# Sparse-expert ranking with four score chunks and four row dots per head, selectors made on VectorE alone, three score chunks per 32 tokens of one-hots

## The reference

```python
def peer(h, w_query, sub_keys, expert_u, expert_v):          # 8 heads, 128 keys, top 16
    qry = (h @ w_query).reshape(B, S, PEER_HEADS, 2, PEER_HALF)
    sc = jnp.einsum('bshpd,hpnd->bshpn', qry, sub_keys)
    top_s, top_i = lax.top_k(sc, K)
    cand = top_s[..., 0, :, None] + top_s[..., 1, None, :]
    best, flat = lax.top_k(cand.reshape(B, S, PEER_HEADS, K * K), K)
    ...
    experts = i1 * 128 + i2                                   # of 16384, 128 per token
    g = softmax(best)
    ...
        act = gelu(einsum('td,tkd->tk', xt, expert_u[et])) * gt
        return einsum('tk,tkd->td', act, expert_v[et])
```

## Time and profile before

| what | us |
|---|---|
| median of 3 runs (1989.82 to 1993.12) | 1991.67 |
| the profiled execution's own time | 1990.13 |
| its span in the profile | 1988.5 |
| TensorE busy (matmuls) | 1825.9, 92% of the span |
| VectorE busy | 1345.9, 68% |
| ScalarE busy | 697.0 |
| GpSimd busy | 649.0 |

### The profile page before, as it was taken

One profiled execution on the slowest core, in us unless ns is written; L12 is line 12 of the kernel. 1 busy time (PEld: TensorE's weight loads), 2 busy tenths in 40 slices (PEclk: granted clock), 3 DMA queues, 4 the chain that ended last, 5 costly groups with the idle time before them and its releaser, 6 DMA issues.

```text
span 1988.5 us, 24521 instructions
## 1 busy us (share of the span) xinstructions
PE 1825.9 (92%) x8747; PEld 1510.3 (76%) x8747; DVE 1345.9 (68%) x2464; ACT 697.0 (35%) x1072; POOL 649.0 (33%) x418
## 2 busy tenths in 40 slices
PE   5899999989979999778888699999999999999996
PEld 4555555558758999777777599999999999877774
DVE  5423233244446999679999487777767888777776
ACT  2241514252334444333333233333333333333333
POOL 0000000000004665676666354444434444322320
PEclk7989888889989999899999899999999999999998
DMA  7413030202313332347888898888878888899992
GB/s 317 169 45 146 21 127 21 84 21 96 111 49 125 124 123 88 117 161 200 218 222 226 243 406 314 309 301 308 310 274 320 318 307 300 312 326 332 325 326 101
DMA packets 217066, 409.64 MB, mean 206 GB/s; under 512 B 111792, under 2 KB 143536, under 8 KB 213040
## 3 DMA queue, kind: packets, MB, share of 16 engines
q1 hardware_dynamic: 170928, 254.56, 37.6%
q0 software_dynamic: 37440, 142.62, 20.9%
q10 hardware_dynamic: 8640, 11.80, 1.6%
HBM read 369.87 MB, written 39.06 MB: 206 GB/s over the span
## 4 chain that ended last, share of the span: by engine, by line
PE 65%; DVE 18%; DMA 6%; issue 4%; ACT 4%; POOL 2%; SPq 1%; DVEq 0%; ACTq 0%; POOLq 0%
PE bank L781 22%; PE bank L725 17%; PE bank L687 6%; DMA u_raw<-euT 4%; PE bank L580 4%; PE bank L621 3%; DVE hot_j L1354 3%; PE bank L615 2%; DVE hot_i L1354 2%; PE bank L584 1%; DVE rows L1335 1%; ACT v_split L1052 1%; PE bank L609 1%; DVE u_split L1330 1%; PE bank L634 1%
## 5 line engine op out<-in xcount | busy, mean ns | idle before, releaser
L725 PE MATMUL bank<-h_split,u_split 128*128 128x384 f32 x3072 | 566.2, 341 | 26.2 <-DVE u_split L1330 15.1
L725 PEld LDWEIGHTS bank<-h_split,u_split 128*128 128x128 f32 x3072 | 545.2, 191 | 33.5 <-DVE u_split L1330 15.4
L781 PE MATMUL bank<-v_split,a_split 128*128 128x512 f32 x2304 | 544.8, 392 | 4.9 <-DVE a_split L1383 3.6
L781 PEld LDWEIGHTS bank<-v_split,a_split 128*128 128x128 f32 x2304 | 427.7, 188 | 104.6 <-issue 18.4
L496 POOL DMA_INDIRECT rows<-ev,idx x128 | 173.7, 1357 | 311.6 <-DVE row_sum L1346 265.5
L496 POOL DMA_INDIRECT rows<-eu,idx x128 | 177.0, 1383 | 232.4 <-DVE dots L1335 212.6
L1052 ACT ACTIVATE v_split<-v_raw 128x1024 fp32r<-128x1024 f32 x128 | 135.8, 1061 | 211.7 <-PE bank L781 208.5
L949 ACT ACTIVATE gelus<-bank 128x384 f32<-128x384 f32 x128 | 62.9, 491 | 388.6 <-PE bank L725 388.5
L1366 DVE TENSOR_TENSOR v_split<-v_raw,v_split 128x1024 fp32r<-128x1024 f32 x128 | 156.6, 1224 | 22.2 <-ACT v_split L1052 22.0
L1335 DVE CUSTOM_DVE_ANT_0 rows<-rows,h_rows 128x1024 f32<-128x1024 f32 x128 | 165.9, 1332 | 0.9 <-DMA rows<-eu,idx 0.8
L1346 DVE SCALAR_TENSOR_TENSOR row_sum<-rows,agate,row_sum 128x1024 f32<-128x1024 f32 x127 | 162.7, 1281 | 5.3 <-DVE row_sum L1346 0.5
(11 more groups left out here) (208 smaller groups left out, 2119.1 us busy)
## 6 DMA issues: line engine op xcount, KB each, us to landing
u_raw<-euT SPq DMA_DIRECT2D x128, 512.0 KB
v_raw<-ev SPq DMA_DIRECT2D x128, 512.0 KB
arena<-w_ada SPq DMA_DIRECT2D x12, 2048.0 KB, 8.0
gates_scratch<-stage SPq DMA_DIRECT2D x12, 2048.0 KB, 17.9
gates<-gates_scratch SPq DMA_DIRECT2D x128, 192.0 KB
arena<-w_units SPq DMA_DIRECT2D x24, 512.0 KB, 3.5
gelu_scratch<-gelus ACTq DMA_DIRECT2D x60, 192.0 KB, 2.0
gelus<-gelu_scratch SPq DMA_DIRECT2D x60, 192.0 KB
```

What stands on the lines that cost most here:

```text
L725: last = pe.matmul(ps[6 + b][:, 0:TD], us[:, b, wp, k * P:(k + 1) * P], hs[:, xp, k, 0:TD], start=(k == 0 and q == 0), stop=(k == DC - 1 a ...
L781: last = pe.matmul(ps[2 * t + f][:], ar[:, b, ap, t * P:(t + 1) * P], vs[:, b, vp, f * 512:(f + 1) * 512], start=(first and q == 0), stop= ...
```

## The change

- Ranking: four score chunks per head instead of three, then four instead of eight (EARLY = 36). The turns go with chunks 0 to 4 rather than heads 0 to 4. The row index is computed head by head (`row_index`), and 28 row dots come early: four ahead of each rank from head 2 on, four after rank 7; their gathers stand on GpSimd at the end of each head from 1 on. VectorE's loop over heads is written out.
- One-hots: GpSimd's multiplication goes. VectorE makes `ohj` by one `tensor_scalar` per token (compare with the index, multiply by the gate, both one scalar per partition), `ohi` as before. Three score chunks, with 3, 3 and 2 groups of four tokens behind them, share 32 tokens: 36 chunks in place of 24. A dot comes in every third. VectorE works five groups ahead. TensorE's loop is written out.
- 76 chunks are stashed instead of 60, so 52 instead of 68 iterations have a new score chunk. 48 dots lie before the values instead of 32, the other 80 in 28 iterations; rows of `expert_v` are added from iteration 29, 64 of them by iteration 52.

```diff
-EARLY = 32
-GSTEPS = TD // 16
-STASHED = EARLY + GSTEPS + 4
+PER_HEAD = 4
+EARLY = PER_HEAD * HEADS + 4
+GROUPS = TD // 4
+BESIDE = 3 * GROUPS // 8
+STASHED = EARLY + BESIDE + 4
-DOTS_G = 32
-DOTS_BY = 38
-ACC_FROM = 39
-ACC_F = 76
+DOTS_HEAD = 4
+DOTS_RANK = DOTS_HEAD * (HEADS - 1)
+DOTS_G = DOTS_RANK + GROUPS // 8 + 8
+DOTS_BY = 28
+ACC_FROM = 29
+ACC_F = 64
+def groups_after(c):
+    k = c - EARLY
+    first = 8 * (k // 3) + 3 * (k % 3)
+    return range(first, first + (3, 3, 2)[k % 3])
...
 @block.sync
+            for n in range(GROUPS // 16):
+                for k in range(6):
+                    u_load(EARLY + RING + 6 * n + k)
+                for b in range(4):
+                    sp.wait_ge(staged[b], 4 * (n + 1) + FREE)
...
 @block.gpsimd
+                if g < P and g % TOPK == 0:
+                    pool.wait_ge(idx_ready, g // TOPK + 1)
...
+                u_low(PER_HEAD * n + 2)
+                u_low(PER_HEAD * n + 3)
                 if n:
                     index_picks(n - 1)
                 if n + 2 < HEADS:
                     query_low(n + 2)
+                u_low(PER_HEAD * n + 4)
+                u_low(PER_HEAD * n + 5)
+                if n:
+                    for k in range(DOTS_HEAD):
+                        gather(DOTS_HEAD * (n - 1) + k)
...
-            for s in range(GSTEPS):
-                for b in range(4):
-                    t0 = 16 * s + 4 * b
-                    pool.wait_ge(hot_eq[b], 2 * s + 2)
-                    nc.gpsimd.tensor_tensor(ohj[:, b, :, :], ohj[:, b, :, :], slotsT[:, 2, t0:t0 + 4].unsqueeze(2).to_broadcast([P, 4, P]),
-                                            ALU.mult).then_inc(hot_ready[b], 1)
-                gather(NG + s)
 @block.tensor
+            for c in range(EARLY, EARLY + BESIDE):
+                scores(c, c % 2)
+                for g in groups_after(c):
+                    b = g % 4
+                    pe.wait_ge(hot_ready[b], g // 4 + 1)
+                    pe.wait_ge(staged[b], g // 4 + FREE)
+                    for q in range(4):
+                        last = pe.matmul(ps[2 + b][:, q * P:(q + 1) * P], ohj[:, b, q, :], ohi[:, b, q, :], start=True, stop=True)
+                    last.then_inc(hot_done[b], 1)
 @block.scalar
+            for c in range(EARLY, EARLY + BESIDE):
+                gelu(c)
+                u_high(c + 2)
+                gelu_stash(c)
+                for g in groups_after(c):
...
 @block.vector
             def rank(i, finish_before=False):
+                if i >= 2:
+                    for k in range(DOTS_HEAD):
+                        dot(DOTS_HEAD * (i - 2) + k)
...
                 if finish_before:
                     finish(i - 1)
+                    row_index(i - 1)
...
+            for i in range(HEADS):
+                rank(i, finish_before=i > 0)
+            for k in range(DOTS_HEAD * (HEADS - 2), DOTS_RANK):
+                dot(k)
             finish(HEADS - 1)
...
+            def hot(g):
+                b = g % 4
+                if g >= 4:
+                    ve.wait_ge(hot_done[b], g // 4)
+                nv.tensor_tensor(ohi[:, b, :, :], cst[:, K_IOTA:K_IOTA + P].unsqueeze(1).to_broadcast([P, 4, P]),
+                                 slotsT[:, 0, 4 * g:4 * g + 4].unsqueeze(2).to_broadcast([P, 4, P]), ALU.is_equal)
+                for q in range(4):
+                    t = 4 * g + q
+                    ins = nv.tensor_scalar(ohj[:, b, q, :], cst[:, K_IOTA:K_IOTA + P], slotsT[:, 1, t:t + 1], slotsT[:, 2, t:t + 1],
+                                           ALU.is_equal, ALU.mult)
+                ins.then_inc(hot_ready[b], 1)
+            for g in range(5):
+                hot(g)
+            ve.wait_ge(u_split, EARLY + 2)
+            for c in range(EARLY, EARLY + BESIDE):
+                u_low(c + 2)
+                if (c - EARLY) % 3 == 2:
+                    dot(DOTS_RANK + (c - EARLY) // 3)
+                for g in groups_after(c):
+                    if g + 5 < GROUPS:
+                        hot(g + 5)
```

More of the change, by code:

```diff
@@ L403, in _ @@
             for n in range(HEADS):
-                u_load(3 * n + 4)
+                u_load(PER_HEAD * n + RING)
                 if n + 2 < HEADS:
@@ L742, in _ @@
                     key_scores(n)
-                scores(3 * n, 3 * n % 2)
-                if n:
-                    key_scores(n)
-                if n < TT:
-                    turn(n, x, n)
-                elif n == TT:
-                    turn(n, h, TT - 1)
-                scores(3 * n + 1, (3 * n + 1) % 2)
-                scores(3 * n + 2, 3 * n % 2)
-            for c in range(3 * HEADS, EARLY):
+                for k in range(PER_HEAD):
+                    c = PER_HEAD * n + k
+                    scores(c, c % 2)
+                    if n and k == 0:
+                        key_scores(n)
+                    if c < TT:
+                        turn(c, x, c)
+                    elif c == TT:
+                        turn(c, h, TT - 1)
+            for c in range(PER_HEAD * HEADS, EARLY):
                 scores(c, c % 2)
@@ L760, in _ @@
                 last.then_inc(slotsT_done, 1)
-            with pe.Fori(0, GSTEPS // 2) as r:
-                for e in range(2):
-                    scores(r * 2 + (EARLY + e), e)
-                    for b in range(4):
-                        pe.wait_ge(hot_ready[b], r * 2 + (e + 1))
-                        pe.wait_ge(staged[b], r * 2 + e + FREE)
-                        for q in range(4):
-                            last = pe.matmul(ps[2 + b][:, q * P:(q + 1) * P], ohj[:, b, q, :], ohi[:, b, q, :], start=True, stop=True)
-                        last.then_inc(hot_done[b], 1)
-            for c in range(EARLY + GSTEPS, STASHED + 1):
+            for c in range(EARLY, EARLY + BESIDE):
+                scores(c, c % 2)
+                for g in groups_after(c):
[5 more added lines that the diff above has]
+                    last.then_inc(hot_done[b], 1)
+            for c in range(EARLY + BESIDE, STASHED + 1):
                 scores(c, c % 2)
@@ L1238, in _, with dot @@
                 nv.tensor_tensor(hs[:, 1, k, :], h[:, k, :], hs[:, 0, k, :].bitcast(F32), ALU.subtract).then_inc(h_split, 1)
+            def dot(k):
+                ve.wait_ge(rows_in[k % NG], 16 * (k // NG + 1))
+                nv.tensor_tensor_reduce(rows[k % NG], rows[k % NG], hT, 1.0, 0.0, ALU.mult, ALU.add, dots[:, k:k + 1]).then_inc(rows_used, 1)
             def finish(i):
@@ L1309, in rank @@
                                      ALU.is_equal).then_inc(picks, 1)
[L1311 to L1315 removed]
+            for i in range(HEADS):
+                rank(i, finish_before=i > 0)
+            for k in range(DOTS_HEAD * (HEADS - 2), DOTS_RANK):
+                dot(k)
             finish(HEADS - 1)
[L1320 removed]
             ve.wait_ge(slots_ready, HEADS)
             nv.tensor_copy(gate3[:], slots[:, 2, TT - 1, :])
[L1323 removed]
+            row_index(HEADS - 1)
             ve.wait_ge(slotsT_ready, 3)
[L1325 removed]
             def u_low(c):
@@ L1330, in u_low @@
                 nv.tensor_tensor(us[:, c % 2, 1, :], ut[:, c % RING, :], us[:, c % 2, 0, :].bitcast(F32), ALU.subtract).then_inc(u_split, 1)
-            def dot(k):
-                ve.wait_ge(rows_in[k % NG], 16 * (k // NG + 1))
-                nv.tensor_tensor_reduce(rows[k % NG], rows[k % NG], hT, 1.0, 0.0, ALU.mult, ALU.add, dots[:, k:k + 1]).then_inc(rows_used, 1)
             def add_row(k):
```

117 lines of the change are left out of this document (40 added, 77 removed).

## The result

| | us |
|---|---|
| before, median of 9 runs | 1991.94 |
| after, median of 9 runs (1995.36 to 2002.02) | 1999.14 |
| ratio after to before, 95% interval | 1.0034 (1.0023 to 1.0045) |
| the profiled execution of after, and its span | 1996.83, 1995.1 |

The account below looks back on a forecast made before the run. TensorE, busy 92%, was taken as the bound, losing 76 us in one-hots paced by VectorE. Stretch ending at 1123.6 with 66.9 us more done than at 1110.6: 53.9 ahead, less 2.9, 51.0; forecast 1941, range 1930 to 1968.

Parts of the forecast that it names:

- Step 1: One-hots: selectors on VectorE alone at 0.26 us each, unit 17.8 us, so TensorE at 19.5 sets the pace.
- Rival A: One-hots: VectorE sets the pace, selectors 0.32 to 0.35 us or held by gathers; 1950 to 1972, chance 0.14.
- Step 2: One-hots: 36 chunks, 235.1 us of work, plus 21 us of TensorE stops behind stage writes; stretch 258.1 us.
- the 2 us for the start: One-hots: 2 us added at their start because u_low(36) stands behind the last index_picks on GpSimd.
- Step 3: Ranking: four chunks per head, VectorE's period 30.5 us (29.4 to 32), slots turned at 865.5, a gain of 1.1.
- four dots at 1.14: Ranking: four early dots per head at 1.14 us each, part of VectorE's 30.5 us period.
- Steps 4 and 5: Values: dots moved forward cost 0 (up to 19 us), at 330 GB/s; sixteen more stashed chunks cost 2.9 us.
- Rival C: Stretch after 1155: DMA limits it, adding 19 us for 1960; chance 0.08.
- Step 6: Tail from 1111 to 1155 stays, with SP's last two writes again ahead of a load.
- D: Ranking: contended dots and gather waits make the period 39.7 us, not 30.5; slower, 2000; chance 0.06.
- E: Loss only moves from one-hots to the ranking's end, VectorE's period near 38, time within 4 us; chance 0.04.
- rival B: One-hots: the stall on the stage writes vanishes, with fewer gathers per round; 1920 to 1930, chance 0.06.

Follow-up runs that it names:

- e5: e3 with one more u_load issued ahead of each pair of stage writes, in the three-chunk order; 1939.47 us, ratio 0.9728.
- e8: Kernel before with selectors on VectorE alone and one u_load moved ahead of each pair of stage writes; 1944.68 us, ratio 0.9763.
- e2: After, with each rank's four dots moved from ahead of it to behind its candidate sums, the last four left in place; 1961.89 us, ratio 0.9861.
- e3: e2 with the last four ranking dots done among the one-hots; 1962.87 us, ratio 0.9851.
- e11: After without early dots in the ranking; 1957.88 us, ratio 0.9829.
- e1: After, with its 28 early dots replaced by a sum over the same row, one SBUF operand instead of two; 1944.04 us, ratio 0.9763.
- e6: e5 without early dots in the ranking; 1930.24 us, ratio 0.9685.

## Why the prediction was wrong, point by point

- **Step 1 (selectors), right.** The 384 `tensor_scalar` take 340 ns in the middle, and four of them in a row 1.11 us, so they start 0.26 us apart, the value that the prediction took. TensorE waits for `hot_j` 2.3 us in all. GpSimd's gathers didn't hold them. Rival A is out.
- **Step 2 (three chunks, and the wait behind the stage writes), right in sum and in mechanism, off in its parts.** The stretch lasted from 922.75 to 1180.37, 257.6 us against 258.1 forecast. In each round there is one ScalarE wait for `u_raw` (7.50 us; 8 to 10 forecast) and a TensorE stop (1.98 and 0.77; 4.2 forecast), and pairs of writes come 42.9 us apart ((1181.37 - 966.68)/5; 43 forecast). e5 and e8 show the cause. By start times a round loses 3.5 us (42.9, less six chunks at 4.25 and 16 groups at 0.87), 17.5 in all and not 21, and the 2 us for the start don't show. What makes up for it was in no term: chunks take 4.25 us from start to start (937.52 - 933.27) rather than 4.18, and after 23 us of idling TensorE starts the stretch at half its clock (0.50 granted from 922 to 925, 0.70 from there to 931), so that its first chunk takes 6.10. That the sum came within 0.5 us is luck in part. Rows of after, of the selectors' line first, then from the timeline:

```profile
L1361 DVE TENSOR_SCALAR hot_j<-cst,slots_turned x384: 329/340/435, 926.9 to 1176.3; 128x128 f32<-128x128 f32 x192
...
991.80 1.06 ACT L944 ACTIVATE u_split<-u_raw 128x1024 fp32r<-128x1024 f32 x1 [7.50 <-DMA u_raw<-euT]
...
993.49 1.13 PE L773 MATMUL bank<-hot_i,hot_j 128*128 128x128 f32 x8 [1.98 <-ACT stage L1040]
1001.34 1.16 PE L773 MATMUL bank<-hot_i,hot_j 128*128 128x128 f32 x8 [0.77 <-DVE hot_j L1361]
1180.37 3.89 PE L729 MATMUL bank<-h_split,u_split 128*128 128x384 f32 x21
```

- **Step 3 (ranking), wrong, and the whole of the miss.** The term that failed is "four dots at 1.14", with its upper bound of 32 us for the period ("if each dot takes 0.4 more"). Measured: 3.85 per dot on average, 15.4 for four, period 38.6. The terms: rank(2) starts 7.7 us late (691.0 for 683.3), five periods bring 5 x 8.1 = 40.5, and the end 9.1 (38.75 from rank(7) to the slots, for 29.7). Per head the dots miss by 10.8 (15.4 for 4.6), but the rank without them takes 23.2 rather than 25.9 (25.7 and 0.2): part of the 25.7 was waiting, 2.0 of it in the copy shown below. "The last four dots stand beside the wait for GpSimd's picks" was wrong too: they stand beside the picks themselves and lengthen them.
- **How the row was misread.** The earlier trace rows gives 1210/1222/2064 for dots. The median is that of dots beside nothing or beside gathers. The prediction took the longest, 2.06, for the price under contention. But those dots only met the tail of a GpSimd operation. The price of meeting one squarely is that operation's whole length, and the earlier trace rows had the pattern: 0.68 became 1.52 beside a 1.25 us multiply. The ranking of before shows it bare, in a copy of four columns that takes 0.15 us by itself (the line's instructions as in the earlier trace rows, then the timeline):

```profile
L1292 DVE COPY arena<-arena x8: 149/2138/2385, 625.1 to 819.7; 128x4 f32<-128x4 f32 x8
743.74 2.21 DVE L1292 COPY arena<-arena 128x4 f32<-128x4 f32 x1
743.54 2.38 POOL L479 TENSOR_TENSOR u_split<-u_raw,u_split 128x1024 fp32r<-128x1024 f32 x1 [5.18 <-ACT u_split L940]
```

The copy starts 0.20 after a `u_low` and ends with it, at 745.95 against 745.92. It also shows that one operand is not always enough to be free: a `tensor_reduce` was, this copy isn't. What was not done is to list what GpSimd runs at the instant at which VectorE reaches the dots. The compare just ahead of them releases it.
- **Steps 4 and 5, right.** From 1226 to 1641 TensorE is busy 415.0 of 415.0 at 329 GB/s (330 forecast), the pairs take 8.31, and values alone 8.6 per two. Rival C is out.
- **Step 6, right within a microsecond:** the tail lasts 45.1 us (44.2 before).
- **The rivals.** D had the size almost exactly: period 39.7, time 2000, and it came on the side "slower". It got there by another sum: dots at 2.06 and VectorE waiting out four gathers. Both halves are wrong (3.4 rather than 2.06; gathers beside dots cost nothing, as e2 shows). The argument against it, that multiplies and not gathers stood beside slow dots, was the right observation, and should have led to the subtractions and multiplies that GpSimd runs in the ranking. E ("period near 38") is the rival that names what happened, the loss moved from the one-hots to the ranking. It had the period, but no mechanism, and 0.04; its time, within 4 us of before, was missed by 3.
- **Open:** why e3 gave back in the one-hots what it gained at the slots. e11's longer stop goes the same way, and both have more gathers there, which the prediction's rival B also supposed; no run varied the gathers alone. Nor is it known what the tail's 0.9 us are. How many dots slip through before the picks is bounded only by two (most do) and four (they don't).

## What to carry to other kernels

Before moving a VectorE instruction with two SBUF operands (or a copy), look up in the timeline what GpSimd runs at its new place: each meeting is paid with the other engine's instruction, up to its full length and on both engines, and a shift by a few microseconds can decide over 50. When one engine's slow step is removed, ask what it covered: the selectors were worth 21 us alone and 48 with the late load mended. And a write that fills a DMA queue delays the loads behind it; put the load that is needed first ahead of the write, unless what follows waits for the write itself.

## What the runs showed of the hardware

- The two engines alternate by whole instructions: dot 1.22 to 3.35 (5.50 beside a 4.6 us operation), GpSimd's 128x1024 `tensor_tensor` 2.40 to 3.3. A `tensor_reduce` of the same row with one operand stays at 1.21 in the same place (e1). A copy of four columns, 0.15 by itself, takes 2.2 beside a `u_low` (before, 743.74).
- Dots beside gathers on GpSimd take 1.22 us, no loss; the gathers take 1.7 to 2.0 rather than 0.94 (e2).
- An `u_load` behind a pair of 2048 KB stage writes holds SP for 10 to 16 us in issue alone (10.5 at 1019.61 in after, 16.3 at 1118.11 in e6), where one otherwise takes 0.33 to 0.44 us.
- TensorE idled for 23 us before the slots were turned in after; the granted clock was 0.50 from 922 to 925, the lower of its two levels (1.2 GHz), and 1.00 from 931 on. The first chunk took 6.10 us for 4.25.
